# A mixture-of-experts layer with a third size class: 96 rows for 24 experts in 44 units instead of 50

## The reference, cut to what matters

```
a = jnp.einsum('td,edh->teh', h, w1)          # 1024 -> 128, 64 experts
b = jnp.einsum('td,edh->teh', h, w3)
act = silu(a) * b * gate[..., None]           # gate is 0 for the experts that a token did not choose
routed = jnp.einsum('teh,ehd->td', act, w2)   # 128 -> 1024
```

## Time and profile before

| | us |
|---|---|
| median of 3 runs | 1427.9 |
| lowest and highest | 1424.88, 1430.07 |
| the profiled execution, device time | 1431.2 |
| its span, first to last instruction | 1429.1 |
| experts of the first layer, from the first product (L1335) to the end of the last (L1357) | 462.75 to 821.46 |
| read-back of the first layer's rows issued | 828.75 |
| experts of the second layer, first transpose | 1125.88 |

### The profile page before, as it was taken

The page is one execution under the profiler, slowest core; times in us unless marked ns, Lnnn a source line. Parts: engine busy times, 40 slices in busy tenths (PEclk is TensorE's granted clock), DMA queues, the critical chain, the costliest instruction groups (busy, mean ns, idle before and its releaser), DMA issues.

```text
span 1429.1 us, 19065 instructions
## 1 busy us (share of the span) xinstructions
PE 1285.2 (90%) x6356; PEld 705.7 (49%) x6357; DVE 544.0 (38%) x1327; ACT 293.5 (21%) x715; POOL 301.1 (21%) x394
## 2 busy tenths in 40 slices
PE   4999998999968999989898969899987799999993
PEld 1443454444534666655565624475544354545441
DVE  5303533554665222223232207455456521211124
ACT  0100114233111222222221211212611111111110
POOL 1001004334123233333332300101710411111110
PEclk9999999999989999999999989999997899999997
DMA  9875309653355999999999379341322999999960
GB/s 334 328 283 191 142 0 267 238 204 119 140 191 211 332 382 377 363 375 370 383 378 390 119 299 364 125 155 25 94 104 83 399 397 392 404 408 398 404 250 31
DMA packets 113083, 373.30 MB, mean 261 GB/s; under 512 B 17978, under 2 KB 24380, under 8 KB 104792
## 3 DMA queue, kind: packets, MB, share of 16 engines
q1 hardware_dynamic: 89112, 313.50, 58.4%
q0 software_dynamic: 23008, 55.40, 10.6%
q10 hardware_dynamic: 864, 3.15, 0.6%
HBM read 368.77 MB, written 30.47 MB: 279 GB/s over the span
## 4 chain that ended last, share of the span: by engine, by line
PE 41%; SPq 12%; DMA 8%; DVE 4%; issue 3%; ACT 1%; POOL 0%; POOLq 0%; DVEq 0%; ACTq 0%
PE bank L1335 11%; SPq L647 10%; PE bank L1357 6%; PE bank L1367 5%; PE bank L943 3%; PE bank L1323 3%; DMA qkv<-in_exp_w 2%; PE bank L1145 2%; PE bank L951 2%; DMA weights<-in_exp_w 2%; DMA probs_T<-in_exp_w 2%; PE bank L1036 1%; PE bank L1026 1%; SPq L778 1%; PE bank L1188 1%
## 5 line engine op out<-in xcount | busy, mean ns | idle before, releaser
L1335 PE MATMUL bank<-weights,b_qk 128*64 128x256 f32 (+2 forms) x1040 | 160.8, 386 | 1.8 <-DVE b_qk L2295 1.5
L1335 PEld LDWEIGHTS bank<-weights,b_qk 128*64 128x64 f32 (+2 forms) x1040 | 110.7, 147 | 62.3 <-issue 34.6
L2301 DVE TENSOR_TENSOR expert_act<-silu_a,bank 128x128 f32<-128x128 f32 x76 | 21.9, 288 | 312.6 <-ACT silu_a L1658 312.6
L1367 PE MATMUL bank<-tokens_h,a_k 128*128 128x512 f32 x208 | 103.5, 622 | 0.0
L2532 POOL DMA_INDIRECT shift_scale_gate_norm<-scratch_h,gather_index x82 | 85.1, 1038 | 70.6 <-POOL gather_index L2529 68.4
L1357 PE MATMUL bank<-weights,expert_act_T 128*64 128x512 f32 (+2 forms) x260 | 91.9, 619 | 8.6 <-DMA weights<-in_exp_w 4.1
L1335 PE MATMUL bank<-features_h,b_qk 128*32 128x256 f32 (+2 forms) x512 | 95.2, 381 | 0.4
L1323 PE MATMUL bank<-tab,shift_scale_gate_norm 128*128 128x128 f32 x624 | 83.0, 276 | 8.4 <-DMA shift_scale_gate_norm<-scratch_h,gather_index 8.4
L1145 PE MATMUL bank<-weights,features_h 128*128 128x512 f32 x192 | 85.9, 602 | 1.3 <-ACT features_h L1445 0.7
L1658 ACT ACTIVATE silu_a<-bank 128x128 f32<-128x128 f32 x76 | 21.1, 278 | 314.7 <-PE bank L1335 314.7
L1323 PEld LDWEIGHTS bank<-tab,shift_scale_gate_norm 128*128 128x128 f32 x624 | 75.9, 191 | 17.6 <-issue 16.9
(11 more groups left out here) (360 smaller groups left out, 1960.4 us busy)
## 6 DMA issues: line engine op xcount, KB each, us to landing
weights<-in_exp_w SPq DMA_DIRECT2D x195, 512.0 KB, 12.1
features_h<-in_exp_w SPq DMA_DIRECT2D x64, 512.0 KB, 11.1
qkv<-in_exp_w SPq DMA_DIRECT2D x64, 512.0 KB, 15.8
shift_scale_gate_norm<-in_ada_w SPq DMA_DIRECT2D x24, 1024.0 KB, 8.8
a_q<-in_exp_w SPq DMA_DIRECT2D x32, 512.0 KB, 13.1
weights<-in_w_in SPq DMA_DIRECT2D x6, 2048.0 KB
shift_scale_gate_norm<-scratch_mod POOLq DMA_DIRECT2D x16, 512.0 KB, 8.7
c_padded<-in_ada_w SPq DMA_DIRECT2D x8, 1024.0 KB, 6.0
```

The lines of the kernel that those rows point to most:

```text
L1335: mm = pe.matmul(ab[r, 0:2 * HIDDEN].rearrange("p (m h) -> p m h", m=2), XGT[:, u.slot() % 2, k, r], expert_w13(slot)[:, :, k, :], start=k ...
L1367: mm = pe.matmul(ACC[g][h][:, :], GROW[:, u.slot() % 2, g * P:(g + 1) * P], YSB[:, u.slot() % 2, h * HALF:(h + 1) * HALF], start=False, st ...
```

## The change

The first layer's experts get a third class. The 30 lightest still share 15 pairs of 64 rows, the next 24 get 96 rows each, and only the last 10 keep a whole unit. Four experts of 96 rows fill three units: unit one holds strips of 64 and 32 rows of expert 0 and one of 32 rows of expert 1, unit two 64 rows of expert 1 and 64 of expert 2, unit three 32 of expert 2, 32 of expert 3 and 64 of expert 3. An expert's weights are loaded once and stay in their slot until its last unit. So there are 15 + 6 x 3 + 10 units and the overflow unit, 44 in all, and still 65 loads. The overflow unit moves from the end to behind the tenth item of the order (`ALWAYS_AT`), and three pairs are held back to be the last units (`LAST_PAIRS`). The order becomes, with P a pair, S a single, T the three units of a group of four, O the overflow unit: P S T P S P S T P S O P T S P P S T P S P S T P S P T S P P P P.

On DVE the capacity and the first slot of each rank are computed for three general classes, and the jump of a row into an overflow unit is now a difference that one instruction takes after the PSUM read (a small one on the counts goes). The second layer's units and their order stay as they are; its DVE instructions change with the first's.

```diff
@@ -46,12 +46,27 @@
 TILES = 4
 STREAMS = ((0, 1), (2, 3))
 FULL = ((0, 1, 2, 3), (2, 3))
-QUADS = (0, 8)
-PAIRS = (15, 14)
-SINGLES = tuple(EXPERTS - 4 * q - 2 * p for q, p in zip(QUADS, PAIRS))
-UNITS = tuple(q + p + f for q, p, f in zip(QUADS, PAIRS, SINGLES))
+QUAD = (tuple((e, slice(32 * e, 32 * e + 32)) for e in range(4)),)
+PAIR = (tuple((e, slice(64 * e, 64 * e + 64)) for e in range(2)),)
+FOUR_IN_THREE = (((0, slice(0, 64)), (0, slice(64, 96)), (1, slice(96, 128))),
+                 ((1, slice(0, 64)), (2, slice(64, 128))),
+                 ((2, slice(0, 32)), (3, slice(32, 64)), (3, slice(64, 128))))
+SINGLE = (((0, slice(0, P)),),)
+CLASSES = (((15, PAIR, 2), (6, FOUR_IN_THREE, 3), (10, SINGLE, 4)),
+           ((8, QUAD, 1), (14, PAIR, 2), (4, SINGLE, 4)))
+
+
+def experts_of(shape):
+
+    return 1 + max(e for unit in shape for e, _ in unit)
+
+
+UNITS = tuple(sum(n * len(shape) for n, shape, _ in classes) for classes in CLASSES)
+BOUNDS = tuple((c[0][0] * experts_of(c[0][1]), c[0][0] * experts_of(c[0][1]) + c[1][0] * experts_of(c[1][1])) for c in CLASSES)
 ALWAYS = (1, 0)
-SHARE = (64, 32)
+ALWAYS_AT = 10
+LAST_PAIRS = (3, 0)
+SHARE = (32, 32)
 UNROLL = 4
 RING = 3
 MASKED = -1e30
@@ -84,22 +99,30 @@
 
 def sequence(l):
 
-    held = SINGLES[l] - UNROLL if l < DEPTH - 1 else SINGLES[l]
-    kinds = [[QUADS[l], 4, 0, 0], [PAIRS[l], 2, QUADS[l], 4 * QUADS[l]],
-             [held, 1, QUADS[l] + PAIRS[l], 4 * QUADS[l] + 2 * PAIRS[l]]]
-    every, order = sum(k[0] for k in kinds), []
+    classes, held = CLASSES[l], LAST_PAIRS[l]
+    many = [n for n, _, _ in classes]
+    kind = [shape for _, shape, _ in classes].index(PAIR)
+    many[kind] -= held
+    every, order = sum(many), []
     for n in range(every):
-        late = [((n + 1) * k[0] / every - order.count(i), i) for i, k in enumerate(kinds)]
+        late = [((n + 1) * k / every - order.count(i), i) for i, k in enumerate(many)]
         order.append(max(late)[1])
-    order += [2] * (SINGLES[l] - held)
-    seq, x, done = [], 0, [0, 0, 0]
-    for i in order:
-        _, many, column, where = kinds[i]
-        seq.append((column + done[i], [(x + j, where + many * done[i] + j) for j in range(many)]))
-        done[i] += 1
-        x += many
-    for n in range(ALWAYS[l]):
-        seq.append((UNITS[l] + n, [(x + n, EXPERTS + n)]))
+    order += [kind] * held
+    column = [0, classes[0][0] * len(classes[0][1])]
+    column.append(column[1] + classes[1][0] * len(classes[1][1]))
+    where = [0, *BOUNDS[l]]
+    seq, x = [], 0
+    for at, i in enumerate(order):
+        shape = classes[i][1]
+        if at == ALWAYS_AT:
+            for n in range(ALWAYS[l]):
+                seq.append((UNITS[l] + n, [(x, EXPERTS + n, slice(0, P))]))
+                x += 1
+        for unit in shape:
+            seq.append((column[i], [(x + e, where[i] + e, r) for e, r in unit]))
+            column[i] += 1
+        x += experts_of(shape)
+        where[i] += experts_of(shape)
     return seq
 
 
@@ -110,7 +133,6 @@
 DIAGONALS = 8
 TABLES = 2 + DEPTH
 EARLY = 3
-STRIPS = {n: tuple(slice(i * P // n, (i + 1) * P // n) for i in range(n)) for n in (1, 2, 4)}
 
 
 def column_of(l, n):
...
@@ -783,7 +805,7 @@
                 loads = EXPERTS + ALWAYS[l]
                 for x in range(loads + W2_LAG):
                     if x < loads:
-                        if x == EXPERTS:
+                        if where[x] >= EXPERTS:
                             sp.wait_ge(list_ready, 2 * l + 2)
                         if x == UNROLL:
                             sp.wait_ge(bank_filled, jobs.filled(("sh", l, FULL[l][-1])))
@@ -1325,13 +1347,12 @@
 
                 def products(u, experts):
 
-                    rows = STRIPS[len(experts)]
-                    for slot, fills in experts:
+                    for slot, fills, _ in experts:
                         pe.wait_ge(L[f"w13_in{slot}"], fills * 32)
                     pe.wait_ge(L["xT_scalar"], u.n(1))
                     pe.wait_ge(L["xT_vector"], u.n(1))
                     for k in range(KD):
-                        for (slot, _), r in zip(experts, rows):
+                        for slot, _, r in experts:
                             mm = pe.matmul(ab[r, 0:2 * HIDDEN].rearrange("p (m h) -> p m h", m=2),
                                            XGT[:, u.slot() % 2, k, r], expert_w13(slot)[:, :, k, :],
                                            start=k == 0, stop=k == KD - 1)
@@ -2160,7 +2180,8 @@
                     shared_act(1, full[1])
 
                 NB16 = RT[:, 11, :].bitcast(BF16)
-                two, four = 4 * QUADS[l], 4 * QUADS[l] + 2 * PAIRS[l]
+                one, (two, four) = CLASSES[l][0][2], BOUNDS[l]
+                more_two, more_four = CLASSES[l][1][2] - one, CLASSES[l][2][2] - CLASSES[l][1][2]
                 count, key, rank, cap, base, over, upto, t0, t1, t2, t3 = (NB1[0:EXPERTS, i:i + 1] for i in range(11))
                 b = filled(("count", l))
                 iota = const("iota_slot")[0:EXPERTS, 0:EXPERTS]
...
@@ -2200,7 +2218,6 @@
                         ALU.is_ge))
                 link(tt(t1, upto, over, ALU.subtract))
                 link(ts(t1, t1, float(P // SHARE[l]), float(P // SHARE[l] * UNITS[l]), ALU.mult, ALU.add))
-                link(tt(t1, t1, t3, ALU.subtract))
                 ts(NB16[0:EXPERTS, 320:384], ident[0:EXPERTS, 0:EXPERTS], t1, None, ALU.mult).then_inc(ends_ready, 1)
                 b = filled(("list", l))
                 drained(("list", l), dve.tensor_copy(LIST[0:1, 0:EXPERTS], b[0:1, 0:EXPERTS]))
@@ -2212,6 +2229,7 @@
                         ALU.min))
                 drained(("over", l), dve.tensor_copy(R(1)[:, 0:2 * EXPERTS], b[:, 128:128 + 2 * EXPERTS]))
                 dve.wait_ge(vector_step, steps[0])
+                free(tt(R(1)[:, EXPERTS:2 * EXPERTS], R(1)[:, EXPERTS:2 * EXPERTS], R(1)[:, 0:EXPERTS], ALU.subtract))
                 link(ts(turns, turns, int(math.log2(UNROLL)), None, ALU.logical_shift_right))
                 link(ts(turns, turns, int(math.log2(UNROLL)), None, ALU.logical_shift_left))
                 dve.nop().then_inc(list_ready, 1)
```

More of the change, by code:

```diff
@@ L763, in _ @@
                 every, ring_n = len(SEQUENCE[l]), RING_X
-                where = {x: w for _, experts in SEQUENCE[l] for x, w in experts}
-                user = {x: n for n, (_, experts) in enumerate(SEQUENCE[l]) for x, _ in experts}
+                where = {x: w for _, experts in SEQUENCE[l] for x, w, _ in experts}
+                user = {x: n for n, (_, experts) in enumerate(SEQUENCE[l]) for x, _, _ in experts}
                 def load_w13(slot, n, gone=None):
@@ L1381, in _ @@
                     u = At(0, n)
-                    was, experts = (experts if n else None), [(x % ring_n, x // ring_n + 1) for x, _ in listed]
+                    was, experts = (experts if n else None), [(x % ring_n, x // ring_n + 1, r) for x, _, r in listed]
                     products(u, experts)
@@ L1406, in _ @@
                             slot, fills = c - every, i + (-(-(EXPERTS + ALWAYS[l] - (c - every)) // ring_n) + 1)
[L1407 removed]
+                            products(u, [(slot, fills, slice(0, P))])
                             act_T(u)
                             tokens_T(At(i, c + 1))
[L1410 to L1411 removed]
+                            second(u, [(slot, fills, slice(0, P))], 0)
+                            second(u, [(slot, fills, slice(0, P))], 1)
                             if summed:
@@ L2173, in _ @@
                 link(stt(RT[0:EXPERTS, 7, 128:128 + EXPERTS], KEY, key, ALL1, ALU.is_lt, ALU.mult, accum_out=rank))
[L2174 to L2185, removed]
+                free(ts(t0, rank, two - 0.5, float(more_two), ALU.is_gt, ALU.mult))
+                free(ts(t1, rank, four - 0.5, float(more_four), ALU.is_gt, ALU.mult))
+                free(ts(t2, rank, -float(two), 0.0, ALU.add, ALU.max))
+                link(ts(t3, rank, -float(four), 0.0, ALU.add, ALU.max))
+                free(stt(cap, t0, float(one), t1, ALU.add, ALU.add))
+                free(ts(base, rank, float(one), None, ALU.mult))
+                link(ts(t2, t2, float(more_two), None, ALU.mult))
+                link(stt(t3, t3, float(more_four), t2, ALU.mult, ALU.add))
+                link(tt(base, base, t3, ALU.add))
                 link(stt(t2, cap, -float(SHARE[l]), count, ALU.mult, ALU.add))
```

## The result

The changed kernel takes 1451.97 us (median of 4 runs, 1450.94 to 1457.05) against 1426.84 us (4 runs) for the kernel before: 1.0177 of it, 95% interval 1.0153 to 1.0202, 25 us slower. Forecast were 1458 us and +30. The profiled execution took 1450.94 us with a span of 1449.1 us; the profiled one of before took 1431.2, so between the two profiles lie 19.7 us, and between the medians 25.1: the profiled execution of before was one of its slower ones, that of the changed kernel the fastest of its four. Ratios in this document leave out two executions of the experiments that fell far from the rest of their kernels, 4,499.78 us of the kernel before and 1,916.22 us of the run with its units and three pairs last, whose median would be 1423.28 without it.

The account below looks back on a forecast made before the run. PE and DMA were both nearly full; with mixed widths PE was taken as the bound: 295.7 + 92 = 388 us against 358.7, +29, plus 0.6 for DVE, about +30 on 1427.9, so 1458 us, range 1404 to 1474.

Parts of the forecast that it names:

- each change of width empties PE: Mixed units' products: strips of 64 and 32 rows run in two groups, each change costing 0.15 us; chance 0.57.
- The rival that gave 1406: First layer's mixed units: different widths run side by side, PE needs 295.7 us, DMA decides, -22 + 0.6 us; chance 0.34.
- The term of the 12 mixed units: First layer's experts: each mixed unit costs 7.7 us more on PE, 92 us for all 12.
- +29: First layer's PE time: 388 us needed against the phase's 358.7 now, with the stalls counted as gone.
- DVE's arithmetic: Rank arithmetic in both layers: more small instructions, +0.5 us in the first and +0.3 in the second, sum +0.6.
- From PE's end to the read-back: End of the first layer's phase: the read-back is issued 7.3 us after PE's end in the kernel before.
- Stalls: First layer's experts: PE would never wait for weights, so 27.6 us of stalls are gone; DMA share clearly below 0.9.
- This moves nothing where PE is the bound: Overflow unit in the middle and pairs last: no effect, since units cost the same at any place.
- Turns without a price: Mixed units: groups take turns but the width change is hidden, -1 us plus 0.6, 1427.5 us; chance 0.05.
- The ring: Weight slots held for three units starve PE; five more 4 us stalls take -22 to about 0; within the remaining 0.04.
- extra turn of overflow units: Rival that more than one overflow block is needed, adding four singles, 26 us; all but excluded, within the remaining 0.04.

Follow-up runs that it names:

- the run with strips of 32: Changed kernel with every 96-row expert cut into strips of 32 rows only, so no unit mixes widths: 1403.89 us, 0.984 of the kernel before.
- the alternating run: The run with strips of 32, plus odd slices of the second layer's pair products done as four strips of 32: 1409.99 us, 0.9875 of the kernel before.

## Why the prediction was right

*The direction and its cause.* Forecast was that strips of 64 and 32 rows take turns and that each change of width empties PE, at a price. The turns are shown by the start of the 64-row strip 0.55 us behind the others on free columns, the price of a change by the period of a slice (0.135 us), by leaving 14 changes of a product out (0.131) and by adding 7 to another (0.144). That PE empties at a change is the reading of a weight load that starts only with the first record after it (495.63), and no run tests it apart from its price. The Trainium skill's rule (TensorEngine Tiling (Array Packing), Key Properties: a change of the mode drains TensorE) agrees with these rows for strips of 64 and 32 columns, and the picture in the Trainium skill of mask bits on each instruction and tiles that overlap (TensorE: Matmul & The Clock Gate, Part 3) holds here only among strips of one width. The price was measured before between units on the same columns, and the prediction says that this could not tell a change of width from occupied columns. That it holds on free columns too was a judgement, put at 0.57 against 0.34, which those rows could not decide.

The rival that gave 1406 was close in the time, 1404 with the mixing taken out, but not in its parts. In the run with strips of 32 the last weights were awaited until 786.7 us and not 797.5, and PE still had 8.4 us to do then, not two halves of a second product; the read-back came at 801 and not 807.

*The sum.* PE for 44 units, mixing aside, was put at 295.7 us. The term of the 12 mixed units was 92 us and measured 86.6 (382.3 - 295.7), 7.2 instead of 7.7 a unit. By parts: a product took 5.4 or 5.2 us more (9.09 - 3.65, 8.84 - 3.65), not 5.7, since a change costs 0.135 and not 0.15; a half of the second product about 0.97 more, not 1.0; 12 products and 24 halves are 64 + 23 = 87. So PE was forecast at 388 us and took 382.3, and +29 became +23.6. One reading behind it was too simple: a half of the second product doesn't take 0.86 us for one strip and 1.01 for two. It is 1.05 for one strip behind a pair's product, and in the changed kernel 0.86 for two where pairs follow pairs (826.37, `x4`). The sum goes by whole units, so this didn't touch it. DVE's arithmetic took 0.61 us more in the first layer and 0.24 more in the second (forecast 0.5 and 0.3); the first of these was reckoned from 0.61 us for the three instructions before, which take 0.43. From PE's end to the read-back it was 5.9 us instead of 7.3, and the first product started 1.6 us earlier; over the profiles of this study it starts between 461.1 and 466.1 without a pattern. That leaves +20.6 us at the read-back, beside the 19.7 between the profiled executions; by medians it is 25. Where these 5 us lie is open, with one profile of each kernel.

*Stalls.* That PE would never wait for weights, and that the DMA share would fall below 0.9, came out as forecast (no wait, 0.88).

*The order.* "This moves nothing where PE is the bound" was right for the changed kernel (382.7 against 382.3 us). What the prediction passed over is that the same order, without the third class, would have made the kernel before 0.6% faster (0.9938). The change buried this gain under the mixed widths.

*Other rivals.* Turns without a price are excluded by the alternating run. The ring set no limit that shows: the run with strips of 32 has the same slots held and runs at a DMA share of 1.01. No extra turn of overflow units ran: the profile has 76 gathers, 44 units and 3 ahead plus 26 and 3.

## What to carry to other kernels

Column strips of TensorE saved time only among strips of one width here (64 and 32 rows; other mixtures inside a unit were not tried). Before mixing widths, cut the wide strip into narrow ones with the same streamed operand: its product took 3.6 us like one of equal strips, and it turned +25 us into -22. If widths must mix, do all of one and then all of the other, and count 0.14 us for each change and the whole streaming of each group. Where two resources are both near full, look at what is left to do when the last transfer lands: an order that ends on the units with the most transfer for their work, with the overflow unit moved forward, was worth 6.5 to 9 us here, without any edit to the units.

## What was not expected of the hardware

With 44 instead of 50 units, and strips of 32 only, the DMA engines moved more in the same time. Between 480 and 780 us the run with strips of 32 had a share of 1.01 and 390 GB/s, the kernel before 0.99 and 377, with the same weights and rows in all. The DMA view of this stretch, of the kernel before and then of that run:

```profile
DMA packets 35442, 113.13 MB, mean 377 GB/s; under 512 B 7878, under 2 KB 7878, under 8 KB 35417
```

```profile
DMA packets 35468, 117.11 MB, mean 390 GB/s; under 512 B 6949, under 2 KB 6949, under 8 KB 35438
```

The number of packets is the same within 0.1%, and fewer of them are small. In the nine runs with a DMA share of 0.98 or more in this stretch, 35,015 to 35,468 packets passed, while the bytes went from 112.2 MB (50 units) to 117.4 (44 units). The small ones come with the gathers and scatters, and not with the rows: over the whole execution the kernel before has 17,978 packets under 512 B and both kernels with 44 units 16,250, at the same 373.3 MB. Six units fewer are thus 1,728 small packets fewer, 144 for each gather and each scatter. That they are the cause of the lower rate was not tried; the changed kernel with its 44 units moved 332 GB/s at a share of 0.88, 377 by the share, against 386 in the run with strips of 32 and 381 before. The higher rate goes with a read-back at 801 instead of the forecast 807.
